# Other element orders for the feed-forward operands of a two-layer transformer kernel

## The chip, the cores and the metric

The kernel runs on one core of one Trainium2 chip. The metric is the device time of one execution in microseconds (us). Below, TensorE is the matrix engine (PE in the profile; PEld is its loading of weights, which overlaps its products), VectorE is DVE, ScalarE is ACT, GpSimd is POOL, and SyncE (SP) issues the transfers.

## The reference

Two layers over 512 tokens of width 1024. Layer 0 mixes tokens by attention over the best keys of an indexer, layer 1 by attention with compressed queries and keys. After each mixer comes the part that the change touches:

```python
def conv_ffn(h, w_up, conv_w, conv_b, w_down):      # h: 512 x 1024
    u = h @ w_up                                     # 512 x 5632
    u = conv_b + sum(conv_w[j] * up[:, j:j + S] for j in range(3))   # three taps along the tokens
    gate, val = jnp.split(u, 2, axis=-1)
    return (jax.nn.silu(gate) * val) @ w_down        # 2816 x 1024
```

All data are 32-bit floats.

## The kernel before

Activations lie with features on the 128 partitions and the 512 tokens along the free dimension. A product must keep more digits than the matrix engine's quick 32-bit form has, so each operand is split in two: an upper part (`w_hi`, `h_hi`, `a_hi`), which ScalarE makes by copying into that form, and a lower part (`w_lo`, `h_lo`, `a_lo`), which VectorE makes by subtracting the upper part from the original. `product3` (L1715 to L1717) then issues three matmuls for one tile, upper by upper, upper by lower and lower by upper, each with its own load of 128x128 weights and 512 moving columns.

Weights arrive in units in two slots of `raw` (SyncE's queue, L389). `hi(u)` (L571) on ScalarE waits for the transfer and for the slot's last use by TensorE, and copies `raw` to `w_hi`. `lo(u)` (L937) on VectorE follows it. TensorE waits for `w_lo_done`. SyncE's load of unit u into `raw` waits until `lo` of unit u - 2 is done.

The feed-forward part of layer `l` has two stretches:

- The up stretch, `feed_forward(l)`: 11 steps. A step takes two units of 2048 words a partition (8 blocks `k` of 256 columns, that is two tiles of 128 for each `k`), and makes four banks of `ps` (`channels`, q = 0 to 3) of 24 matmuls each. VectorE scales each bank (L1165), ScalarE and VectorE apply the taps (L786, L1172, L1177), ScalarE the silu (L807), and VectorE multiplies (L1198). In the middle steps, `hi` and `lo` of the next step's slot 0 stand behind the scaling of banks 0 and 1, those of slot 1 behind the rest of the step. The first step is written apart.
- The down stretch, `onto_residual(n, ...)` with n = 1 in layer 0 and n = 3 in layer 1: 22 units of 1024 words a partition, 8 tiles each; `tile_product` for tile `d` goes to bank `d`, so a unit has 24 matmuls. For each later unit ScalarE makes `w_hi` and `a_hi` (L733) as soon as unit u - 2 is used (`r_used`), VectorE `w_lo` and `a_lo` (L1106), and TensorE waits for both lower parts before the unit's first product.

Behind the last unit of the down stretch of layer 0, ScalarE waits for the transfer of the next stage's weights (`raw<-in_b_w_down`) and converts their second half (L761), VectorE subtracts it (L1135), and in program order behind that stand VectorE's additions of the eight banks to `xT` (L1139) and the next stage's features (`h_hi` L579, `h_lo` L943).

Of the kernel before, what the change touches and what calls it, by code (L numbers as in the profile page):

```python
# [21 lines left out]
F32 = mybir.dt.float32  # L22
F32R = mybir.dt.float32r
BF16 = mybir.dt.bfloat16
ALU = mybir.AluOpType
# [3 lines left out]
P = 128  # L29
# [86 lines left out]
def unit_words(u):  # L116

    if u < U_AOUT:
        return 4 * A_CHUNKS[(u - U_A) // 2][1]
    if u < U_UP[0]:  # L120
        return D
    if u < U_DOWN[0]:
        return SLOT
    if u < U_B:
        return D
    if u < U_BOUT:
        return (4 * B_DOWN, 4 * B_DOWN, QW, QW, D, D)[u - U_B]
    if u < U_UP[1]:
        return D
    return SLOT if u < U_DOWN[1] else D  # L130


def score_bank(u, e):
# [30 lines left out]
def hybrid_layers_kernel(nc, xt, vectors, t5_bias, a_in_wide, a_in_small, a_w_out, b_w_down, b_w_uq,  # L164
# [4 lines left out]
    with ExitStack() as ctx:  # L169
# [391 lines left out]
        def _(sc):  # L561
            chain = Chain(sc, act_seq)

            def hi(u, free=None, n=None, k=None):
# [187 lines left out]
            def onto_residual(n, u0, tiles, n_next, gain_at, nxt):  # L752

                with sc.Fori(0, tiles // 2 - 1) as i:
                    for b in range(2):
                        hi(u0 + 2 * i + b + 2, (r_used[n], 2 * i + b + 1), D, b)
                        act_hi(n, 2 * i + b + 2, b, False)
                if n_next < 4:
                    half = unit_words(nxt) // 2
                    sc.wait_ge(w_raw[0], 8 * nxt + 16)  # L760
                    sc.activation(w_hi[:, 0, D:D + half], raw[:, 0, D:D + half], ACT.Copy).then_inc(w_hi_upper, 1)  # L761
                    order = ORDER[n_next]
                    for j, k in enumerate(order):
                        features_hi(n_next, k, gain_at)
                        if j >= 2:
                            square_of(n_next, order[j - 2])
                        if j == KD - 2:
                            hi(nxt, (r_done[n], KD), half)
                    for k in order[-2:]:
                        square_of(n_next, k)  # L770
                    hi(nxt + 1, (r_done[n], KD))
                    if nxt == U_B:
                        table(ACT.Sqrt)
                        hi(U_B + 2, (pb_half, 1))
                    root_of_mean(n_next)

            def feed_forward(l):
                n = 2 * l + 1

                def tap2(i, q, first):  # L780

                    ch = l * CT + (q // 2) * FT + 2 * i + q % 2
                    sc.wait_ge(f_in[l], 4 * i + q + 1)
                    if not first:
                        sc.wait_ge(f_act[l], 2 * i)
                    sc.activation(cv[:, q, :], u_in[:, q, 2:2 + S], ACT.Identity,  # L786
                                  bias=conv[:, 3, bass.ds(ch, 1)], scale=conv[:, 2, bass.ds(ch, 1)])\
                        .then_inc(f_t2[l], 1)

                def step(i, first=False, last=False):  # L790
                    if first:
                        hi(U_UP[l] + 2, (f_done[l], 2))
                        sc.wait_ge(bc_ok, l + 1)
                        sc.activation(rbc[:], ps[:, 1, :], ACT.Copy).then_inc(rbc_ok, 1)
                    tap2(i, 0, first)
                    tap2(i, 1, first)
                    if first:
                        pass
                    elif last:
                        hi(U_DOWN[l], (f_done[l], 4 * i + 2))  # L800
                        act_hi(n, 0, 0, True)
                        act_hi(n, 1, 1, True)
                    else:
                        hi(U_UP[l] + 2 * i + 2, (f_done[l], 4 * i + 2), SLOT, 0)
                    for q in range(2):
                        sc.wait_ge(f_t0[l], 4 * i + q + 1)
                        sc.activation(cv[:, q, :], cv[:, q, :], ACT.Silu).then_inc(f_silu[l], 1)  # L807
                    tap2(i, 2, first)
                    tap2(i, 3, first)
                    if last:  # L810
                        hi(U_DOWN[l] + 1, (f_done[l], 4 * i + 4))
                    else:
                        hi(U_UP[l] + 2 * i + 3, (f_done[l], 4 * i + 4), SLOT, 1)
# [110 lines left out]
        def _(dve):  # L924
            chain = Chain(dve, dve_seq)

            def lo(u, n=None, k=None):
# [9 lines left out]
                dve.tensor_tensor(w_lo[:, s, 0:n], raw[:, s, 0:n], w_hi[:, s, 0:n].bitcast(F32), ALU.subtract)\  # L937
                    .then_inc(w_lo_done, 1)

            def prepare_lo(n, k, gain_at):  # L940

# [184 lines left out]
            def onto_residual(n, u0, tiles, n_next, gain_at, nxt):  # L1126
                with dve.Fori(0, tiles // 2 - 1) as i:
                    for b in range(2):
                        lo(u0 + 2 * i + b + 2, D, b)
# [21 lines left out]
            def feed_forward(l):  # L1151
                n = 2 * l + 1
                for t in range(T):
                    dve.tensor_scalar(diag[:, t, :], ident, rstd[:, t:t + 1], None, ALU.mult)\
                        .then_inc(diag_ok, 1)
                lo(U_UP[l] + 2)
                chain.then_wait(dve.memset(u_in[:, :, 0:2], 0.0))
                dve.wait_ge(rbc_ok, l + 1)

# [20 lines left out]
                def ffn_step(i, first=False, last=False):  # L1180
                    scaled(i, 0, first)
                    scaled(i, 1, first)
                    if first:
                        pass
                    elif last:
                        lo(U_DOWN[l])
                        act_lo(n, 0, 0)
                        act_lo(n, 1, 1)
                    else:
                        lo(U_UP[l] + 2 * i + 2, SLOT, 0)  # L1190
                    taps(i, (0, 1))
                    scaled(i, 2, first)
                    scaled(i, 3, first)
                    taps(i, (2, 3))
                    dve.wait_ge(f_t0[l], 4 * i + 4)
                    for q in range(2):
                        dve.wait_ge(f_silu[l], 2 * i + q + 1)
                        dve.tensor_tensor(act[:, 2 * i + q, :], cv[:, q, :], cv[:, 2 + q, :], ALU.mult)\  # L1198
                            .then_inc(f_act[l], 1)
                    if last:  # L1200
                        lo(U_DOWN[l] + 1)
                    else:
                        lo(U_UP[l] + 2 * i + 3, SLOT, 1)

                ffn_step(0, first=True)
                with dve.Fori(1, UP_STEPS - 1) as i:
# [114 lines left out]
        def _(pe):  # L1321
# [176 lines left out]
                if j == 2:  # L1498
                    ins.then_inc(o_ok[n], 1)

            def tile_product(d, b, start, stop):
# [26 lines left out]
            def onto_residual(n, u0, tiles):  # L1528

                def rows(i, first=False):  # L1530
                    for b in range(2):
                        pe.wait_ge(w_lo_done, u0 + 2 * i + b + 1)
                        pe.wait_ge(r_lo[n], 2 * i + b + 1)
                        for d in range(KD) if n % 2 or not first else (4, 5, 6, 7):
# [7 lines left out]
                            ins = tile_product(d, b, first and b == 0, False)  # L1542
                        ins.then_inc(r_used[n], 1)

                rows(0, first=True)
# [3 lines left out]
                pe.wait_ge(w_lo_done, u0 + tiles - 1)  # L1549
                pe.wait_ge(r_lo[n], tiles - 1)  # L1550
                for d in ORDER[n + 1][:AHEAD]:
                    tile_product(d, 0, False, False)
                pe.wait_ge(w_lo_done, u0 + tiles)
                pe.wait_ge(r_lo[n], tiles)
                for j, d in enumerate(ORDER[n + 1]):
                    if j >= AHEAD:
                        tile_product(d, 0, False, False)
                    tile_product(d, 1, False, True).then_inc(r_done[n], 1)

            def feed_forward(l):  # L1560
                n = 2 * l + 1

                def channels(i, q, first):
# [4 lines left out]
                        pe.wait_ge(f_in[l], 4 * i + q - 3)  # L1568
                    for k in range(KD):
                        cols = slice(k * 2 * P + part * P, k * 2 * P + (part + 1) * P)  # L1570
                        ins = product3(pe, ps[:, 4 + q, :], w_hi[:, s, cols], w_lo[:, s, cols], h_hi[:, k, :],
                                       h_lo[:, k, :], k == 0, k == KD - 1)
                    ins.then_inc(f_done[l], 1)


# [208 lines left out]
```

## Time and profile before

| | |
|---|---|
| time, median of 3 runs | 1264.58 us (1263.28 to 1265.5) |
| span of the profiled execution, first to last instruction | 1259.6 us |
| mean granted TensorE clock of it | 0.996 of full speed |
| busy: PE, PEld | 1220.7 us (97%), 980.3 us (78%) |
| busy: DVE, ACT, POOL | 767.4 us (61%), 547.5 us (43%), 212.6 us (17%) |
| up stretches, layer 0 and layer 1 | about 324 to 561 us, 899 to 1135 us of the span |
| down stretches, layer 0 and layer 1 | about 561 to 682 us, 1135 to 1256 us |

The page gives the profiled execution's span and no time of its own beside it. The span is 5.0 us under the median of the runs; that difference is what lies before the first and behind the last instruction, and is taken as fixed. A matmul's busy time in the profile includes the time that its results take to drain, so consecutive matmuls overlap, and the distance between their starts is the pace.

### The profile page before, as it was taken

The numbers are of one execution on the slowest core, as the hardware profiler recorded it, in microseconds if no ns is written. First come the engines' busy times: TensorE is split into PE (matmuls) and PEld (weight loads), VectorE is DVE, ScalarE is ACT, GpSimd is POOL, SyncE is SP. The second block draws the span as 40 slices with busy tenths as digits, with TensorE's granted clock in tenths as the row PEclk, the third lists the DMA queues.
The fourth block names the chain that finished last, engine by engine and source line by source line (L and its number), as shares of the span: only waits on it lengthen the run. The fifth ranks groups of instructions, "written<-read, shape, count | busy, mean of one in ns | idle before, by whom it ended". The sixth has DMA issues, their size and how long they took to land.

```text
span 1259.6 us, 17234 instructions
## 1 busy us (share of the span) xinstructions
PE 1220.7 (97%) x6072; PEld 980.3 (78%) x6080; DVE 767.4 (61%) x1337; ACT 547.5 (43%) x933; POOL 212.6 (17%) x262
## 2 busy tenths in 40 slices
PE   6999999999999999999999878999999999999998
PEld 4868886678788888888888766768788888887887
DVE  3577895754766666563337678762775666664334
ACT  5554435653633333332325676652543333343232
POOL 4314243430400000000003572430400000000000
PEclk9999999999999999999999999999999999999999
DMA  6432212204222232213332110012322222222323
GB/s 232 155 98 87 96 68 68 73 29 134 100 100 100 76 107 84 100 50 100 100 100 97 59 35 1 1 35 90 113 99 100 100 100 100 74 75 84 100 89 111
DMA packets 25120, 110.83 MB, mean 88 GB/s; under 512 B 2752, under 2 KB 3136, under 8 KB 17776
## 3 DMA queue, kind: packets, MB, share of 16 engines
q1 hardware_dynamic: 25072, 110.21, 25.8%
q8 instruction: 28, 0.46, 0.1%
q14 instruction: 20, 0.16, 0.0%
HBM read 108.06 MB, written 6.33 MB: 91 GB/s over the span
## 4 chain that ended last, share of the span: by engine, by line
PE 86%; DVE 6%; POOL 2%; ACT 2%; issue 2%; DMA 1%; SPq 0%; DVEq 0%; ACTq 0%; POOLq 0%
PE ps L1715 24%; PE ps L1717 24%; PE ps L1716 24%; PE ps L1476 3%; PE ps L1495 3%; PE ps L1376 2%; PE ps L1364 2%; DVE h_lo L943 1%; DVE xT L1139 1%; PE ps L1459 1%; DVE w_lo L937 1%; PE ps L1449 1%; PE ps L1359 1%; DMA xT<-in_xt 1%; POOL rope_tmp L479 1%
## 5 line engine op out<-in xcount | busy, mean ns | idle before, releaser
L937 DVE TENSOR_TENSOR w_lo<-raw,w_hi 128x1024 fp32r<-128x1024 f32 (+4 forms) x114 | 194.7, 1708 | 255.1 <-ACT w_hi L571 255.1
L1715 PE MATMUL ps<-h_hi,w_hi 128*128 128x512 f32 (+1 forms) x712 | 278.4, 391 | 2.4 <-DVE w_lo L937 2.4
L1716 PE MATMUL ps<-h_lo,w_hi 128*128 128x512 f32 (+1 forms) x712 | 277.7, 390 | 0.0
L571 ACT ACTIVATE w_hi<-raw 128x1024 fp32r<-128x1024 f32 (+4 forms) x124 | 177.7, 1433 | 229.8 <-PE ps L1717 229.5
L1717 PE MATMUL ps<-h_hi,w_lo 128*128 128x512 f32 (+1 forms) x712 | 277.5, 390 | 0.0
L1715 PE MATMUL ps<-a_hi,w_hi 128*128 128x512 f32 x480 | 188.0, 392 | 2.1 <-DVE w_lo L937 1.5
L1716 PE MATMUL ps<-a_lo,w_hi 128*128 128x512 f32 x480 | 186.8, 389 | 0.0
L1717 PE MATMUL ps<-a_hi,w_lo 128*128 128x512 f32 x480 | 186.8, 389 | 0.0
L1715 PEld LDWEIGHTS ps<-h_hi,w_hi 128*128 128x128 f32 (+1 forms) x712 | 133.5, 188 | 31.8 <-DVE w_lo L937 3.2
L1717 PEld LDWEIGHTS ps<-h_hi,w_lo 128*128 128x128 f32 (+1 forms) x712 | 133.6, 188 | 28.6 <-issue 0.6
L1716 PEld LDWEIGHTS ps<-h_lo,w_hi 128*128 128x128 f32 (+1 forms) x712 | 133.6, 188 | 28.1 <-issue 0.4
L786 ACT ACTIVATE cv<-u_in,vec 128x512 f32<-128x512 f32 x88 | 71.5, 816 | 187.4 <-DVE u_in L1165 185.4
L501 POOL TENSOR_TENSOR v<-v 128x512 f32<-128x512 f32 x28 | 50.7, 1810 | 462.5 <-ACT v L583 442.6
L1165 DVE TENSOR_TENSOR u_in<-ps,rbc 128x512 f32<-128x512 f32 x88 | 60.2, 688 | 94.3 <-PE ps L1717 91.5
L1715 PEld LDWEIGHTS ps<-a_hi,w_hi 128*128 128x128 f32 x480 | 90.1, 188 | 23.8 <-DVE w_lo L937 2.4
L1717 PEld LDWEIGHTS ps<-a_hi,w_lo 128*128 128x128 f32 x480 | 90.1, 188 | 18.8
L1716 PEld LDWEIGHTS ps<-a_lo,w_hi 128*128 128x128 f32 x480 | 90.1, 188 | 18.3
L1715 PE MATMUL ps<-w_hi,h_hi 128*128 128x512 f32 (+1 forms) x256 | 102.0, 398 | 2.4 <-DVE w_lo L937 1.9
L1717 PE MATMUL ps<-w_hi,h_lo 128*128 128x512 f32 (+1 forms) x256 | 99.5, 389 | 0.0
L1716 PE MATMUL ps<-w_lo,h_hi 128*128 128x512 f32 (+1 forms) x256 | 99.0, 387 | 0.0
L520 POOL TENSOR_SCALAR probs<-probs,inv_sum 128x256 f32<-128x256 f32 (+3 forms) x128 | 66.8, 538 | 106.7 <-DVE inv_sum L1024 106.5
L664 ACT ACTIVATE probs<-probs,neg_max 128x256 f32<-128x256 f32 (+3 forms) x128 | 70.5, 553 | 18.6 <-DVE neg_max L1014 18.4
(189 smaller groups left out, 1525.3 us busy)
## 6 DMA issues: line engine op xcount, KB each, us to landing
raw<-in_f_up SPq DMA_DIRECT2D x44, 1024.0 KB, 4.8
raw<-in_f_w_down SPq DMA_DIRECT2D x44, 512.0 KB, 3.4
raw<-in_a_in_wide SPq DMA_DIRECT2D x13, 1024.0 KB, 4.9
bias_tiles<-bias_rows SPq DMA_DIRECT2D x1, 4096.0 KB, 20.1
raw<-in_a_w_out SPq DMA_DIRECT2D x8, 512.0 KB, 3.4
raw<-in_b_w_out SPq DMA_DIRECT2D x8, 512.0 KB, 3.4
xT<-in_xt SPq DMA_DIRECT2D x4, 512.0 KB, 6.3
toep_b<-bias_tiles SPq DMA_DIRECT2D x8, 256.0 KB, 2.8
```

The costliest lines, as they stand in the source:

```text
L501: pool.tensor_tensor(total, total, sq[:, ORDER[n][k], :], ALU.add).then_inc(sq_sum, 1)
L520: ins = pool.tensor_scalar(x, x, inv_sum[:, slot, e, p:p + 1], 1.0, ALU.mult, ALU.mult)
L571: sc.activation(w_hi[:, s, 0:n], raw[:, s, 0:n], ACT.Copy).then_inc(w_hi_done, 1)
L664: ins = sc.activation(x, x, ACT.Exp, bias=neg_max[:, slot, e, p:p + 1], scale=-1.0, accum_out=sums[:, slot, e, p:p + 1])
L786: sc.activation(cv[:, q, :], u_in[:, q, 2:2 + S], ACT.Identity, bias=conv[:, 3, bass.ds(ch, 1)], scale=conv[:, 2, bass.ds(ch, 1)])\
L937: dve.tensor_tensor(w_lo[:, s, 0:n], raw[:, s, 0:n], w_hi[:, s, 0:n].bitcast(F32), ALU.subtract)\
L1165: dve.tensor_tensor(u_in[:, q, 2:2 + S], ps[:, 4 + q, :], rbc[:], ALU.mult).then_inc(f_in[l], 1)
L1476: ins = pe.transpose(ps[:, turn_bank(u, e), c * P:(c + 1) * P], probs[slot][:, e, c * P:(c + 1) * P], ident)
L1495: ins = pe.matmul(ps[e * DH:(e + 1) * DH, 7, b * P:(b + 1) * P], v[:, kb, h * DH:(h + 1) * DH], probsT[u % 2][:, e, c * P:(c + 1) * P], st ...
L1715: pe.matmul(dst, s_hi, m_hi, start=start, stop=False)
L1716: pe.matmul(dst, s_hi, m_lo, start=False, stop=False)
L1717: return pe.matmul(dst, s_lo, m_hi, start=False, stop=stop)
```

## The change

Three of the four feed-forward stretches read or write their operands in another order. The numbers computed are the same, and the instructions are as many as before.

- Up stretch of layer 0, from the second step: each matmul walks its 512 moving columns from the last to the first, and the bank of `ps` as well.
- Down stretch of layer 0: `hi` and `lo` write `w_hi` and `w_lo` so that column c of tile d stands at word 8c + d. Both read `raw` in order; VectorE reads `w_hi` and writes `w_lo` 8 words apart, ScalarE writes `w_hi` 8 words apart, and TensorE loads each tile's 128 columns 8 words apart.
- Up stretch of layer 1, from the second step: the two tiles of each block k are interleaved, so that column c of tile h stands at word 2c + h of the block. The same accesses are 2 words apart.
- Down stretch of layer 1, first steps of both up stretches, and all else: unchanged.

```diff
+def by_eights(x):
+    return x.rearrange("p (c d) -> p d c", d=KD)
+def by_pairs(x):
+    return x.rearrange("p (k c h) -> p k h c", h=2, c=P)
+def as_stored(x):
+    return x.rearrange("p (k h c) -> p k h c", h=2, c=P)
+def tiles_of(x):
+    return x.rearrange("p (a c) -> p a c", c=P)
+def down_view(n):
+    return (by_eights, tiles_of) if n == 1 else (None, None)
+def up_view(l):
+    return (by_pairs, as_stored) if l == 1 else (None, None)
...
             def hi(u, free=None, n=None, k=None, view=None, of=None):
...
-                sc.activation(w_hi[:, s, 0:n], raw[:, s, 0:n], ACT.Copy).then_inc(w_hi_done, 1)
+                to, source = w_hi[:, s, 0:n], raw[:, s, 0:n]
+                if view is not None:
+                    to, source = view(to), of(source)
+                sc.activation(to, source, ACT.Copy).then_inc(w_hi_done, 1)
...
             def lo(u, n=None, k=None, view=None, of=None):
...
+                to, source, less = w_lo[:, s, 0:n], raw[:, s, 0:n], w_hi[:, s, 0:n].bitcast(F32)
+                if view is not None:
+                    to, source, less = view(to), of(source), view(less)
+                dve.tensor_tensor(to, source, less, ALU.subtract).then_inc(w_lo_done, 1)
...
             def tile_product(d, b, start, stop, n=0):
                 cols = slice(d * P, (d + 1) * P)
+                if n == 1:
+                    cols = slice(d, D, KD)
...
                     for k in range(KD):
                         cols = slice(k * 2 * P + part * P, k * 2 * P + (part + 1) * P)
+                        if l == 1 and not first:
+                            cols = slice(k * 2 * P + part, (k + 1) * 2 * P, 2)
+                        bank, h_upper, h_lower = ps[:, 4 + q, :], h_hi[:, k, :], h_lo[:, k, :]
+                        if l == 0 and not first:
+                            bank, h_upper, h_lower = bank[:, ::-1], h_upper[:, ::-1], h_lower[:, ::-1]
```

The calls of `hi` and `lo` for the units of these stretches pass `*down_view(n)` or `*up_view(l)`.

## Rows read from the trace of the kernel before

**Rows 1.** The page: busy time by engine, and granted TensorE clock in 40 slices.

```profile
PE 1220.7 (97%) x6072; PEld 980.3 (78%) x6080; DVE 767.4 (61%) x1337; ACT 547.5 (43%) x933; POOL 212.6 (17%) x262
...
PEclk9999999999999999999999999999999999999999
```

**Rows 2.** The chain that ended last, shares of the span by engine.

```profile
PE 86%; DVE 6%; POOL 2%; ACT 2%; issue 2%; DMA 1%; SPq 0%; DVEq 0%; ACTq 0%; POOLq 0%
```

**Rows 3.** Windows within the three changed stretches: busy (count), clock, DMA, GB/s.

```profile
346.50:550.50 204.00, 204.00 (x902) 168.92 (x901) 129.12 (x151) 74.91 (x74) 0.00 (x0) 1.00 0.27 93
567.50:659.50 92.00, 92.00 (x406) 76.16 (x407) 31.06 (x34) 26.11 (x34) 0.00 (x0) 1.00 0.32 100
920.90:1124.90 204.00, 204.00 (x902) 168.92 (x901) 129.12 (x151) 74.90 (x74) 0.00 (x0) 1.00 0.26 93
```

**Rows 4.** Timeline, end of one down unit: start, duration, instruction.

```profile
605.48 0.39 PE L1717 MATMUL ps<-a_hi,w_lo 128*128 128x512 f32 x1
605.48 0.19 PEld L1715 LDWEIGHTS ps<-a_hi,w_hi 128*128 128x128 f32 x1
605.70 0.39 PE L1715 MATMUL ps<-a_hi,w_hi 128*128 128x512 f32 x1
```

**Rows 5.** Timeline, matmuls of 384 moving columns at full clock.

```profile
722.51 0.33 PE L1715 MATMUL ps<-w_hi,cq_hi 128*128 128x384 f32 x1
722.68 0.33 PE L1716 MATMUL ps<-w_lo,cq_hi 128*128 128x384 f32 x1
```

**Rows 6.** Timeline, eight weight loads whose matmuls have one column.

```profile
30.78 0.97 PEld L1329 LDWEIGHTS ps<-ones,v 128*128 128x128 f32 x8 [2.00 <-issue]
```

**Rows 7.** Timeline, matmuls of 416 columns while the granted clock was halved.

```profile
689.87 0.55 PE L1717 MATMUL ps<-w_hi,h_lo 128*128 128x416 f32 x1
690.22 0.55 PE L1715 MATMUL ps<-w_hi,h_hi 128*128 128x416 f32 x1
```

**Rows 8.** Groups by line and form: busy us, mean ns, idle before.

```profile
L937 DVE TENSOR_TENSOR w_lo<-raw,w_hi 128x2048 fp32r<-128x2048 f32 x45 | 105.4, 2342 | 58.0 <-ACT w_hi L571 58.0
L571 ACT ACTIVATE w_hi<-raw 128x2048 fp32r<-128x2048 f32 x55 | 104.7, 1904 | 23.3 <-PE ps L1717 23.0 <-DVE rstd L949 0.2
...
L937 DVE TENSOR_TENSOR w_lo<-raw,w_hi 128x1024 fp32r<-128x1024 f32 x63 | 79.8, 1267 | 193.6 <-ACT w_hi L571 193.6
...
L571 ACT ACTIVATE w_hi<-raw 128x1024 fp32r<-128x1024 f32 x63 | 66.7, 1059 | 202.4 <-PE ps L1717 202.4
...
L527 POOL TENSOR_TENSOR w_lo<-raw,w_hi 128x2048 fp32r<-128x2048 f32 x10 | 46.1, 4610 | 90.9 <-ACT w_hi L571 90.9
```

**Rows 9.** Timeline, conversion of one down unit of layer 0.

```profile
600.46 1.06 ACT L571 ACTIVATE w_hi<-raw 128x1024 fp32r<-128x1024 f32 x1 [3.80 <-PE ps L1717]
...
602.70 0.69 DVE L1106 TENSOR_TENSOR a_lo<-act,a_hi 128x512 fp32r<-128x512 f32 x1
```

**Rows 10.** Timeline, the second unit of the down stretch of layer 0.

```profile
566.20 1.22 DVE L937 TENSOR_TENSOR w_lo<-raw,w_hi 128x1024 fp32r<-128x1024 f32 x1
...
567.47 0.50 PE L1715 MATMUL ps<-a_hi,w_hi 128*128 128x512 f32 x1 [0.77 <-DVE w_lo L937]
```

**Rows 11.** The chain in order of time, end of the down stretch of layer 0.

```profile
665.74 1.07 ACT w_hi L571
...
666.84 1.24 DVE w_lo L937
...
668.09 5.22 DMA raw<-in_b_w_down
...
674.27 1.03 DVE w_lo L1135
```

**Rows 12.** Timeline, slot 1 in a middle step of an up stretch.

```profile
436.08 2.29 DVE L937 TENSOR_TENSOR w_lo<-raw,w_hi 128x2048 fp32r<-128x2048 f32 x1
...
441.19 0.19 PEld L1715 LDWEIGHTS ps<-h_hi,w_hi 128*128 128x128 f32 x1
```

More of the change, by code:

```diff
@@ L562, in _, with hi @@
             chain = Chain(sc, act_seq)
-            def hi(u, free=None, n=None, k=None):
+            def hi(u, free=None, n=None, k=None, view=None, of=None):
                 s = u % 2 if k is None else k
@@ L791, in step @@
                     if first:
-                        hi(U_UP[l] + 2, (f_done[l], 2))
+                        hi(U_UP[l] + 2, (f_done[l], 2), None, None, *up_view(l))
                         sc.wait_ge(bc_ok, l + 1)
@@ L810, in step @@
                     if last:
-                        hi(U_DOWN[l] + 1, (f_done[l], 4 * i + 4))
+                        hi(U_DOWN[l] + 1, (f_done[l], 4 * i + 4), None, None, *down_view(n))
                     else:
-                        hi(U_UP[l] + 2 * i + 3, (f_done[l], 4 * i + 4), SLOT, 1)
+                        hi(U_UP[l] + 2 * i + 3, (f_done[l], 4 * i + 4), SLOT, 1, *up_view(l))
                 step(0, first=True)
@@ L925, in _, with lo @@
             chain = Chain(dve, dve_seq)
-            def lo(u, n=None, k=None):
+            def lo(u, n=None, k=None, view=None, of=None):
                 if isinstance(u, int):
@@ L1155, in feed_forward @@
                         .then_inc(diag_ok, 1)
-                lo(U_UP[l] + 2)
+                lo(U_UP[l] + 2, None, None, *up_view(l))
                 chain.then_wait(dve.memset(u_in[:, :, 0:2], 0.0))
@@ L1185, in ffn_step @@
                     elif last:
-                        lo(U_DOWN[l])
+                        lo(U_DOWN[l], None, None, *down_view(n))
                         act_lo(n, 0, 0)
@@ L1189, in ffn_step @@
                     else:
-                        lo(U_UP[l] + 2 * i + 2, SLOT, 0)
+                        lo(U_UP[l] + 2 * i + 2, SLOT, 0, *up_view(l))
                     taps(i, (0, 1))
@@ L1200, in ffn_step @@
                     if last:
-                        lo(U_DOWN[l] + 1)
+                        lo(U_DOWN[l] + 1, None, None, *down_view(n))
                     else:
-                        lo(U_UP[l] + 2 * i + 3, SLOT, 1)
+                        lo(U_UP[l] + 2 * i + 3, SLOT, 1, *up_view(l))
                 ffn_step(0, first=True)
@@ L1541, in rows @@
                                 pe.wait_ge(f_in[n // 2], 2 * FT)
-                            ins = tile_product(d, b, first and b == 0, False)
+                            ins = tile_product(d, b, first and b == 0, False, n)
                         ins.then_inc(r_used[n], 1)
@@ L1551, in onto_residual @@
                 for d in ORDER[n + 1][:AHEAD]:
-                    tile_product(d, 0, False, False)
+                    tile_product(d, 0, False, False, n)
                 pe.wait_ge(w_lo_done, u0 + tiles)
@@ L1556, in onto_residual @@
                     if j >= AHEAD:
-                        tile_product(d, 0, False, False)
-                    tile_product(d, 1, False, True).then_inc(r_done[n], 1)
+                        tile_product(d, 0, False, False, n)
+                    tile_product(d, 1, False, True, n).then_inc(r_done[n], 1)
             def feed_forward(l):
@@ L1570, in channels @@
                         cols = slice(k * 2 * P + part * P, k * 2 * P + (part + 1) * P)
-                        ins = product3(pe, ps[:, 4 + q, :], w_hi[:, s, cols], w_lo[:, s, cols], h_hi[:, k, :],
-                                       h_lo[:, k, :], k == 0, k == KD - 1)
+                        if l == 1 and not first:
[3 more added lines that the diff above has]
+                            bank, h_upper, h_lower = bank[:, ::-1], h_upper[:, ::-1], h_lower[:, ::-1]
+                        ins = product3(pe, bank, w_hi[:, s, cols], w_lo[:, s, cols], h_upper, h_lower, k == 0,
+                                       k == KD - 1)
                     ins.then_inc(f_done[l], 1)
```

12 lines of the change are left out of this document (5 added, 7 removed).

## The prediction

> **What bounds the kernel now.** I first read the page's busy times and its clock row. TensorE is busy for 97% of the span at the upper level of its clock, 2.4 GHz [rows 1]. The chain that ended last says the same: 86% of it is TensorE [rows 2]. I then asked for windows inside the three changed stretches. TensorE is busy without a gap in each, VectorE 63% of the time in an up stretch and 34% in the down stretch, ScalarE less [rows 3]. So a layout can cost time in two ways only: it slows the matmuls or their loads, which all lie on the path, or it slows ScalarE's and VectorE's conversions so far that TensorE waits.
>
> The pace of TensorE is the distance between two starts: 605.70 - 605.48, read over a window as 92.0 us / 406 = 0.227 us [rows 3, 4]. With 384 columns it is about 0.173 us [rows 5], so a column costs (0.227 - 0.173) / 128 = 0.42 ns and 512 of them 0.216 us. About 0.01 us is left, which does not depend on the columns. The loads run beside this. Eight loads whose matmuls have a single column take 0.97 us, the last of them 0.19 us long: (0.97 - 0.19) / 7 = 0.111 us for a load of 128 columns when nothing else sets the pace [rows 6]. A load therefore has half of each 0.227 us to spare.
>
> **The change, part by part.** No instruction is added. No operand in this kernel's on-chip work is read or written backward or with single words apart, so the trace has no row for any of the three patterns, and each is bounded from rows.
>
> *Backward walk, layer 0 up.* Ten steps of 4 banks of 24 matmuls are 960. Lower bound: nothing, if the same words in the opposite order come at the same pace. Upper bound: one word where two came before. The nearest row is the stretch at half clock, where starts lie 0.35 us apart for 416 columns, 0.84 ns a column [rows 7]. That is twice 0.42 ns, so +0.216 us a matmul and 960 x 0.216 = +207 us. I take nothing: every word is still next to the one before it, and the row nearest in kind is the forward walk of the same words. No gain can come of it beyond the 0.01 us above.
>
> *Loads 8 words apart, layer 0 down.* 22 units of 24 are 528 loads. If the load takes as long as now, or even twice as long (0.223 us), it stays under 0.227 us and costs nothing [rows 4, 6]. Three times is 0.334 us, +0.107 us each, +57 us; four times 0.445 us, +115 us. I take at most twice, so 0, knowing that only 0.004 us is left over.
>
> The Trainium skill (Advanced Engine Details and Errata, section Memory Cachelines) says that on-chip memory is read in lines of 16 bytes, that at least two accesses must fall in one line to hide its latency, and that one line per access costs something; it gives no figure for it. No row here shows that. It is a warning about the 8-word pattern for all three engines and leaves out the 2-word one.
>
> *Conversions 8 words apart, layer 0 down.* ScalarE takes 1904 ns for 2048 words and 1059 ns for 1024, so 0.825 ns a word; VectorE 2342 and 1267 ns, so 1.05 ns [rows 8]. Lower bound: unchanged. For the upper side the only other price of this subtraction is GpSimd's, 4610 ns for 2048 words, twice VectorE's [rows 8]. I take twice a word's time on both: +0.84 us for `hi`, +1.07 us for `lo` (between unchanged and twice I choose twice, since each access leaves the words beside it unused; this is a choice, not a reading). In the steady units this is hidden, barely. Now `hi` starts at 600.46 and `a_lo` ends at 603.39 [rows 9]; the later times of the change are 603.39 + 0.84 + 1.07 = 605.30, and the first load of the unit stands at 605.48 [rows 4]. What remains is 0.2 us a unit. Two places have no such cover:
>
> - The second unit. TensorE already waits for its `w_lo`, 0.77 us, and `hi` was done long before [rows 10]. A longer `lo` goes straight on the path: +1.1 us.
> - The last-but-one unit. There the chain is `hi`, `lo`, then the transfer for the next stage into the slot just freed, then L761 and L1135, behind which VectorE's additions stand [rows 11]. `hi` and `lo` both count: +1.9 us. The additions and features after it run back to back on VectorE, so nothing gives it back.
>
> *Two words apart, layer 1 up.* Loads: even doubled they would hide as above. Conversions: unchanged at the lower bound. At the upper bound, doubled, `hi` of 2048 words takes 1.7 us more and `lo` 2.15 us more, twice a step. VectorE would be late by 3.8 us after slot 0, make up 1.7 us of it in its wait before the last bank, and end slot 1's `lo` at 438.4 + 2.1 + 2.1 = 442.6 where TensorE's load wants it at 441.19 [rows 12]: 1.4 us a step, +14 us over ten. I take nothing, as two words apart is nearer to the rows (one apart) than eight.
>
> *Sum.* 0 + 0 + 1.1 + 1.9 + 0 = +3.0 us on the profiled span of 1259.6 us, so 1262.6 us. The span stands 5.0 us under the median of the runs; 1264.6 + 3.0 = **1267.6 us**.
>
> **The rivals.**
>
> *No cost at all.* If ScalarE and VectorE do not notice the spacing either, the sum is 0: 1264.6 us. The rows speak neither for nor against it. It is also what comes of any edit that has no effect in the hardware.
>
> *A small miss.* Three mechanisms lie close. If the 0.01 us that is left over in the pace comes on top of a doubled load, the pace is 0.236 us and 528 x 0.009 = +5 us. If the conversions exceed double, the 0.2 us of cover in each of 20 units is used up, and each further 0.1 us costs 2 us. If 2-word writes are charged, up to +14 us. Together with the +3.0 this is 1269 to 1283 us.
>
> *Loads take over the down stretch.* Above 2.04 times their present 0.111 us they set the pace. With three to four times it is 1267.6 + 57 to 115 = 1325 to 1383 us. Against it: nothing in the rows. For it: the margin is 2%.
>
> *The backward walk halves the pace.* 1267.6 + 207 = 1475 us. This needs an engine that takes words in pairs only forward. The walk at 0.42 ns a word is twice as fast as any other engine's stream here (0.825 and 1.05 ns, and 0.84 ns for a load, rows 6 and 8), so it is where pairs would be needed. The Trainium skill (the same page and section) says of the matmul's results that every two in succession should be adjacent and that an order that is not contiguous slows matmuls significantly; by that the backward bank is at risk, if "contiguous" means ascending. No row here shows it.
>
> *Both, or something worse.* Over 1480 us.
>
> *Faster.* If part of the 0.01 us beside the columns came from loads and walk reaching for the same words' neighbourhood, another order could free it: up to 528 x 0.01 = 5 us. Nothing points to it.
>
> **How the numbers follow.** Forecast 0.27; no cost 0.16; small miss 0.16; loads 0.12; backward 0.20; both or worse 0.07; faster 0.02. The forecast is the likeliest single case, with a range of its own of 1265.5 to 1269.5 us. To hold 8 in 10 the range must reach the backward walk, since all cases below it hold only 0.71 to 0.73. So it is 1263.5 to 1477 us. The bound of 0.2% is 2.5 us. Slower by more: two thirds of the forecast's case (0.18), and all of the small miss, loads, backward and both (0.55), 0.73. Within: no cost and the rest of the forecast's, 0.25. Faster 0.02.
>
> **What would show each step.** The backward walk: the count of matmuls in a 204 us window of layer 0's up stretch, 902 now [rows 3], 460 if halved, with the granted clock still 1.00. The loads: the count in the down window, 406 now, and the duration of a load beside it, 0.19 us [rows 4]; with a doubled load about 0.3 us and the pace unchanged. The conversions: L571 of 1024 words at 1.9 us and L937 at 2.3 us in layer 0's down stretch, 1.06 and 1.23 us still in layer 1's. The two stalls: TensorE's wait of 0.77 us at the second unit grown to 1.8 us, and 1.9 us more between the last-but-one unit's use and the first `xT` addition. Two words apart: L571 and L937 of 2048 words in layer 1 as in layer 0. The prediction is wrong if TensorE's pace changes in any stretch, or if the steady units of the down stretch show a wait for `w_lo`.

## The result

The changed kernel takes 1285.78 us (median of four runs, 1283.84 to 1287.76) where the kernel before takes 1263.93 us (median of four, the three of the table above and one more). The ratio is 1.0175, 95% interval 1.0162 to 1.0189: slower by 1.6 to 1.9%. The profiled spans are 1282.1 and 1259.6 us, 22.5 us apart. In each run that has both on record the time is about 1.8 us above the span (1283.84 over 1282.1 here). The 5.0 us of the section on the time before set one execution's span beside the median of others; the differences used below do not depend on it.

The page of the changed kernel, busy times, chain and clock, answers to [rows 1, 2]:

```profile
PE 1243.5 (97%) x6080; PEld 1015.2 (79%) x6080; DVE 791.1 (62%) x1337; ACT 574.4 (45%) x933; POOL 212.6 (17%) x262
...
PEclk9999999999999999999999999999999999999999
...
PE 88%; DVE 6%; POOL 2%; issue 2%; ACT 1%; DMA 0%; SPq 0%; DVEq 0%; ACTq 0%; POOLq 0%
```

TensorE issues as many matmuls as before (the profile before lacks 8 of the 6080 records) and is busy 22.8 us longer (1243.5 - 1220.7), at the same clock. So most of the time is in its pace. Windows of the four stretches of the changed kernel (busy us and count by engine, granted clock, DMA share, GB/s), for layer 0 up, layer 0 down, layer 1 up, layer 1 down:

```profile
350.00:550.00 200.00, 200.00 (x859) 161.15 (x858) 122.00 (x144) 73.20 (x72) 0.00 (x0) 1.00 0.26 92
580.00:680.00 100.00, 100.00 (x410) 100.00 (x410) 48.53 (x34) 45.17 (x34) 0.00 (x0) 1.00 0.26 86
945.00:1145.00 200.00, 200.00 (x859) 165.44 (x858) 123.85 (x144) 76.38 (x72) 0.00 (x0) 1.00 0.25 89
1165.00:1265.00 100.00, 100.00 (x443) 82.79 (x442) 33.90 (x38) 28.60 (x37) 0.00 (x0) 1.00 0.30 100
```

The second number in each line is TensorE's: in none of these windows is it idle. The count tells the pace. The unchanged stretch makes 443 matmuls in 100 us, 0.227 us each, as [rows 3] have it. The backward stretch and the one with operands 2 words apart (the pairs) both make 859 in 200 us, 0.233 us; the one with operands 8 words apart (the eights) makes 410 in 100 us, 0.244 us. In the down stretch of layer 0 the loads (the third number) are busy for all of the window. From the starts of the matmuls one after the other the means are 226.67 ns in the unchanged stretch, 233.33 backward, 233.33 for the pairs and 244.67 for the eights.

The same stretches by line, changed kernel; first layer 0 down, then layer 1 up (count | busy us, mean ns | idle before), answering to [rows 8]:

```profile
L1759 PEld LDWEIGHTS ps<-a_hi,w_lo 128*128 128x128 f32 x150 | 49.7, 331 | 0.0
...
L973 DVE TENSOR_TENSOR w_lo<-raw,w_hi 128x1024 fp32r<-128x1024 f32 x19 | 43.1, 2268 | 59.1 <-ACT w_hi L604 59.1
L604 ACT ACTIVATE w_hi<-raw 128x1024 fp32r<-128x1024 f32 x19 | 42.3, 2229 | 62.9 <-PE ps L1759 62.9
...
L1757 PEld LDWEIGHTS ps<-h_hi,w_hi 128*128 128x128 f32 x279 | 53.8, 193 | 11.3
...
L973 DVE TENSOR_TENSOR w_lo<-raw,w_hi 128x2048 fp32r<-128x2048 f32 x17 | 38.9, 2290 | 26.7 <-ACT w_hi L604 26.7
L604 ACT ACTIVATE w_hi<-raw 128x2048 fp32r<-128x2048 f32 x18 | 37.3, 2072 | 0.0
```

A load 8 words apart is recorded at 331 ns against 188, one 2 words apart at 193. The conversions 8 words apart have about doubled. Those 2 words apart cost ScalarE 9% and VectorE nothing. Timeline of the changed kernel at the two ends of the down stretch of layer 0 (in brackets the idle time before and what ended it), answering to [rows 10, 11]:

```profile
574.47 0.64 PE L1757 MATMUL ps<-a_hi,w_hi 128*128 128x512 f32 x1 [1.21 <-DVE w_lo L973]
...
690.84 0.68 DVE L1141 TENSOR_TENSOR a_lo<-act,a_hi 128x512 fp32r<-128x512 f32 x1
...
691.67 0.60 PE L1757 MATMUL ps<-a_hi,w_hi 128*128 128x512 f32 x1 [1.56 <-DVE a_lo L1141]
...
692.80 1.42 DVE L1174 TENSOR_TENSOR xT<-xT,ps 128x512 f32<-128x512 f32 x2 [0.34 <-PE ps L1759]
```

The first wait was 0.77 us and is 1.21. The second is new: the last unit's `a_lo` is late, and TensorE, which by then has only five tiles of the unit before (15 matmuls) to work on, waits 1.56 us for it. VectorE's additions to `xT` (last line) then wait 0.34 us for TensorE, not the other way round.

**Where the 22.5 us are.** Up stretch of layer 0: 960 x 6.67 ns = 6.4 us. Down stretch of layer 0: it runs from its first to its last matmul in 120.6 us before and 132.5 us after, +11.9; 528 x 18.0 ns = 9.5 us of that is pace, the rest the two waits. The stage behind it is 2.0 us shorter (162.96 us before, 161.00 after, from last to first matmul of the stretches beside it), all of it within its first 14 us. TensorE's wait there is shorter, and behind it the granted clock was at its lower level, 1.2 GHz, for 3.4 us before [rows 7] and not after. The lines are that wait before, then in the changed kernel:

```profile
688.48 0.45 PE L1715 MATMUL ps<-w_hi,h_hi 128*128 128x416 f32 x1 [1.93 <-DVE w_lo L937]
...
706.02 0.46 PE L1757 MATMUL ps<-w_hi,h_hi 128*128 128x416 f32 x1 [1.40 <-DVE w_lo L973]
```

This gain of 2.0 us goes with the late conversions. Of the kernels of the next section the eights alone gain 2.0 us at this place and the conversions alone 1.5 us, both without the drop of the clock; the backward walk alone, the pairs alone and the loads alone have the drop and gain nothing. Why the drop stays away is open. Up stretch of layer 1: 6.4 us. The sum, 6.4 + 11.9 - 2.0 + 6.4 = 22.7 us, agrees with 22.5.

### The profile page after: what moved, and what is told of

The parts are those of the page before. It is cut to its first block, busy times and chain, and to the rows that moved or that the text cites. A ratio compares the mean times of both kernels' runs of the same rounds, so it can differ in the third digit from the quotient of the medians.

```text
span 1282.1 us, 17242 instructions
## 1 busy us (share of the span) xinstructions
PE 1243.5 (97%) x6080; PEld 1015.2 (79%) x6080; DVE 791.1 (62%) x1337; ACT 574.4 (45%) x933; POOL 212.6 (17%) x262
## 4 chain that ended last, share of the span: by engine, by line
PE 88%; DVE 6%; POOL 2%; issue 2%; ACT 1%; DMA 0%; SPq 0%; DVEq 0%; ACTq 0%; POOLq 0%
PE ps L1757 25%; PE ps L1759 24%; PE ps L1758 24%; PE ps L1511 3%; PE ps L1530 3%; PE ps L1411 2%; PE ps L1399 2%; DVE h_lo L978 1%; DVE xT L1174 1%; PE ps L1494 1%; DVE w_lo L973 1%; PE ps L1394 1%; PE ps L1484 1%; POOL rope_tmp L509 1%; PE ps L1729 1%
## 5 line engine op out<-in xcount | busy, mean ns | idle before, releaser
L973 DVE TENSOR_TENSOR w_lo<-raw,w_hi 128x1024 fp32r<-128x1024 f32 (+4 forms) x114 | 218.2, 1914 | 245.3 <-ACT w_hi L604 245.2
L604 ACT ACTIVATE w_hi<-raw 128x1024 fp32r<-128x1024 f32 (+4 forms) x124 | 206.6, 1666 | 215.9 <-PE ps L1759 215.7
L1757 PE MATMUL ps<-h_hi,w_hi 128*128 128x512 f32 (+1 forms) x712 | 283.1, 398 | 2.4 <-DVE w_lo L973 2.4
L1758 PE MATMUL ps<-h_lo,w_hi 128*128 128x512 f32 (+1 forms) x712 | 282.4, 397 | 0.0
L1759 PE MATMUL ps<-h_hi,w_lo 128*128 128x512 f32 (+1 forms) x712 | 282.3, 396 | 0.0
L1757 PE MATMUL ps<-a_hi,w_hi 128*128 128x512 f32 x480 | 191.4, 399 | 4.1 <-DVE a_lo L1141 2.2
L1758 PE MATMUL ps<-a_lo,w_hi 128*128 128x512 f32 x480 | 190.3, 396 | 0.0
L1757 PEld LDWEIGHTS ps<-a_hi,w_hi 128*128 128x128 f32 x480 | 114.9, 239 | 18.9 <-DVE w_lo L973 4.6
L1759 PEld LDWEIGHTS ps<-a_hi,w_lo 128*128 128x128 f32 x480 | 115.3, 240 | 12.1
L1758 PEld LDWEIGHTS ps<-a_lo,w_hi 128*128 128x128 f32 x480 | 115.2, 240 | 11.5
```

Source lines behind the costliest of these rows:

```text
L604: sc.activation(to, source, ACT.Copy).then_inc(w_hi_done, 1)
L973: dve.tensor_tensor(to, source, less, ALU.subtract).then_inc(w_lo_done, 1)
L1757: pe.matmul(dst, s_hi, m_hi, start=start, stop=False)
L1758: pe.matmul(dst, s_hi, m_lo, start=False, stop=False)
L1759: return pe.matmul(dst, s_lo, m_hi, start=False, stop=stop)
```

## The experiments

**One pattern at a time.** The first three kernels keep one pattern each and set the others back, as this for the first:

```diff
-    return (by_eights, tiles_of) if n == 1 else (None, None)
+    return (None, None)
-    return (by_pairs, as_stored) if l == 1 else (None, None)
+    return (None, None)
-                if n == 1:
-                    cols = slice(d, D, KD)
-                        if l == 1 and not first:
-                            cols = slice(k * 2 * P + part, (k + 1) * 2 * P, 2)
```

> Theory A (each pattern costs TensorE a small amount per matmul, and the amounts add): the pace in the middle steps of layer 0's up stretch is 233.3 ns against 226.7, all other stretches are at 226.7; 960 x 6.67 ns = +6.4 us, so 1270 us. Rival B (the pace rises through something the three edits share, such as the longer program or more crowded memory): with two of three edits gone the backward stretch loses some or all of its 6.67 ns, and the time is 1264 to 1268 us.

Measured: 1.0048 of the kernel before (1.0032 to 1.0063), 1269.23 us. The pace is 233.33 ns in the backward stretch and 226.67 elsewhere. Windows of layer 0's up and down stretches:

```profile
350.00:550.00 200.00, 200.00 (x859) 161.15 (x858) 122.03 (x144) 73.23 (x72) 0.00 (x0) 1.00 0.26 92
580.00:680.00 100.00, 100.00 (x443) 82.79 (x442) 34.50 (x38) 29.39 (x38) 0.00 (x0) 1.00 0.30 98
```

> Theory A: the pace of layer 0's down stretch is 244.7 ns, elsewhere 226.7; 528 x 18.0 ns = +9.5 us, and two stalls of 0.4 us at the second unit and about 1.7 us at the last, less up to 2 us that the next stage may give back: 1273 to 1276 us. Rival B: the pace is nearer to 226.7 ns with the other edits gone.

Measured: 1.0069 (1.0052 to 1.0086), 1272.16 us, 0.8 us under the expected range. The pace is 244.2 ns in layer 0's down stretch, 226.67 elsewhere. Window of layer 0's down stretch:

```profile
580.00:680.00 100.00, 100.00 (x411) 100.00 (x411) 48.62 (x35) 45.52 (x34) 0.00 (x0) 1.00 0.28 89
```

> Theory A: the pace in the middle steps of layer 1's up stretch is 233.3 ns, elsewhere 226.7; +6.4 us, 1270 us, no new stalls. Rival B: 1264 to 1267 us.

Measured: 1.0056 (1.0039 to 1.0073), 1269.76 us. The pace is 233.3 ns in layer 1's up stretch, 226.67 elsewhere. Window of layer 1's up stretch:

```profile
945.00:1145.00 200.00, 200.00 (x859) 165.43 (x858) 122.65 (x145) 74.80 (x75) 0.00 (x0) 1.00 0.25 87
```

The three add up, 0.48 + 0.69 + 0.56 = 1.73% against 1.75%, each known to 0.15 to 0.17%. Theory A stands, rival B falls: each pattern pays in its own stretch, whatever the others do.

**Loads or conversions.** This kernel spaces only TensorE's loads. It and the six kernels after it compute something else than the reference (other columns or tokens, or a part of them) and ran once each, so they are read for paces and durations within their profiles more than for their times.

```diff
+                        if l == 0 and not first:
+                            at = 4 * P * (k // 2) + 2 * (k % 2) + part
+                            cols = slice(at, 4 * P * (k // 2 + 1), 4)
                         if l == 1 and not first:
+                            cols = slice(2 * k + part, SLOT, 16)
...
+                if n == 3:
+                    cols = slice(2 * P * (d // 2) + d % 2, 2 * P * (d // 2 + 1), 2)
```

> The conversions write in order and the walks are forward; only the loads are spaced: 4 words in layer 0's up stretch, 8 in its down stretch, 16 in layer 1's up stretch, 2 in its down stretch. The products then take other weight columns than the reference. Theory C (the loads alone make the pace): 244.7 ns at 8 words and 233.3 at 2, with loads of 331 and 193 ns. If what counts is that each word is alone in a line of 16 bytes, 4, 8 and 16 words give one and the same pace, 244.7 ns; if the cost grows with the distance, 4 words lie between 233.3 and 244.7 and 16 above. Rival D (the spaced writes of ScalarE and VectorE crowd the memory that TensorE reads): all four stretches stay at 226.7 ns.

Measured: 1291.0 us. Windows of this kernel for 4, 8, 16 and 2 words:

```profile
350.00:550.00 200.00, 200.00 (x852) 200.00 (x852) 120.81 (x142) 73.32 (x72) 0.00 (x0) 1.00 0.26 92
580.00:680.00 100.00, 100.00 (x411) 100.00 (x410) 31.06 (x34) 26.86 (x34) 0.00 (x0) 1.00 0.27 89
945.00:1145.00 200.00, 200.00 (x847) 200.00 (x846) 121.36 (x143) 72.54 (x71) 0.00 (x0) 1.00 0.25 90
1165.00:1265.00 100.00, 99.39 (x426) 81.91 (x426) 34.31 (x39) 28.18 (x36) 0.00 (x0) 1.00 0.28 95
```

The mean distances are 235.0, 244.7, 236.5 and 233.3 ns, the last outside a wait in its window. So the loads alone make the pace, and rival D falls. Neither form of theory C holds as written. From 2 to 4 words the recorded load jumps from 193 to 310 ns; it is 331 ns at 8 and 300 ns at 16. That step fits a load that is long once each word is alone in 16 bytes, but 8 words is worse than 4 and 16. Why 8 is worst stays open. The Trainium skill (Advanced Engine Details and Errata, section Memory Cachelines) says that on-chip memory has lines of 16 bytes and that at least two accesses must fall in one line to hide its latency; the step of the recorded load between 2 and 4 words is where it puts it, and the further difference between 4, 8 and 16 is not in it. For moving columns it does not hold: two of them 2 words apart share a line, and they already double a matmul, as measured below.

This kernel also prices the waits: its down stretch of layer 0 takes 129.7 us against the changed kernel's 132.5, so the late conversions there cost 2.8 us.

**Is the load itself the bound?** Two kernels narrow the matmuls, leaving out the other columns of each bank.

```diff
+                        if not first:
+                            bank, h_upper, h_lower = bank[:, 0:256], h_upper[:, 0:256], h_lower[:, 0:256]
...
+                some = slice(0, 256 if n % 2 else S)
```

> The changed matmuls have 256 moving columns instead of 512 (half of each bank is left out). Layer 0 up: backward; layer 0 down: loads 8 words apart; layer 1 up: loads 2 words apart; layer 1 down: in order. In order the pace is 106.7 + 13.3 = 120 ns. If the cost of the backward walk is fixed per matmul, layer 0 up is at 126.7 ns; if it is by the column, 123.3. The same two numbers for loads 2 words apart. Loads 8 words apart: if a load takes 0.218 us by itself, that is now the pace, or a little more; if the cost was a fixed 18 ns, 138 ns.

Measured: 1133.19 us. The windows of layer 0 down (8 words) and layer 1 down (in order, with some waits of TensorE in it):

```profile
540.00:620.00 80.00, 80.00 (x334) 80.00 (x333) 25.57 (x28) 22.10 (x28) 0.00 (x0) 1.00 0.26 89
1080.00:1100.00 20.00, 19.41 (x157) 18.80 (x157) 12.14 (x14) 10.16 (x14) 0.00 (x0) 1.00 0.51 179
```

In order the distance between starts is 120 ns outside the waits, as expected. With loads 8 words apart it is 241 ns, though the matmul is half as wide. The load is the bound. It takes 241 ns by itself, not the 0.218 or 0.223 us of a plain doubling. Backward, 256 columns have a mean of 118.5 ns, and with loads 2 words apart 120.1 (both where TensorE neither waits nor is at the lower clock, which it is for short pieces of these two stretches): at this width neither costs anything.

The same with 64 columns and loads 4, 3, 16 and 1 words apart:

> The changed matmuls have 64 moving columns instead of 512 (the rest of each bank is left out), so that the loads set the pace, and the loads are 4 words apart in layer 0's up stretch, 3 words in its down stretch, 16 in layer 1's up stretch and in order in its down stretch; conversions are in order. In order: 0.111 us a load, as for one column. If a spaced load reads its 128 columns at half the pace, 4 and 16 words give 0.218 us, and the 235 to 245 ns of the full stretches are the load plus something of 17 to 27 ns. If 4 and 16 words give less than 0.15 us, the load is not the bound and the added 8 to 18 ns come from a clash with the moving columns. 3 words (two words in one line of four, then one) should lie between, near 0.165 us.

Measured: 1245.46 us. It does not settle what a load costs by itself at full clock, as its windows for 4, 3, 16 and 1 words show:

```profile
400.00:500.00 100.00, 100.00 (x430) 100.00 (x430) 60.68 (x71) 37.19 (x37) 0.00 (x0) 0.50 0.26 94
580.00:640.00 60.00, 60.00 (x283) 60.00 (x282) 21.91 (x24) 17.84 (x23) 0.00 (x0) 0.50 0.30 104
950.00:1050.00 100.00, 100.00 (x460) 100.00 (x459) 67.36 (x78) 38.85 (x38) 0.00 (x0) 0.50 0.26 94
1140.00:1200.00 60.00, 60.00 (x283) 60.00 (x282) 21.07 (x24) 17.83 (x23) 0.00 (x0) 0.50 0.31 105
```

The granted clock (third number from the end) is 0.50: TensorE fell to 1.2 GHz and stayed there for 327 and 314 us, while it issued loads and 64-column matmuls without a gap. So these paces aren't comparable with the others. Within the kernel they are: at half clock a load in order takes 213 ns, 3 words apart the same, 4 words 233 and 16 words 218.6. At full clock and 512 columns the paces at 4 and 16 words were 235.0 and 236.5 ns, so these loads take no longer at half the clock. That suggests that something other than TensorE's clock bounds them. It is not shown: what a load 4 or 16 words apart takes by itself at full clock was not measured, and loads 8 words apart were not run at half clock.

**Which walk costs.** One walk is changed in each stretch, all else in order:

```diff
                         if l == 0 and not first:
+                            h_upper, h_lower = h_upper[:, ::-1], h_lower[:, ::-1]
+                        if l == 1 and not first:
+                            bank, h_upper, h_lower = in_runs(bank, 2), apart(h_upper, 2), apart(h_lower, 2)
...
                 if n == 1:
+                    bank = bank[:, ::-1]
+                if n == 3:
+                    bank, a_upper, a_lower = in_runs(bank, 4), apart(a_upper, 4), apart(a_lower, 4)
```

> Everything is stored and loaded in order; one walk is changed in each stretch, so the outputs are those of tokens in another order. Layer 0 up: the moving columns backward, the bank forward. Layer 0 down: the bank backward, the moving columns forward. Layer 1 up: moving columns 2 words apart (even ones, then odd ones). Layer 1 down: moving columns 4 words apart. If the read of the moving columns costs the 6.67 ns of the backward stretch, layer 0 up is at 233.3 ns and layer 0 down at 226.7; if the write of the bank costs it, the other way round; if each costs half, 230 in both. If the moving read suffers from spacing as the loads do, 2 words cost little and 4 words (one word of each 16 bytes) up to double the pace, 440 ns; if it only suffers a fixed amount, both are at 233.3.

Measured: 1608.06 us. Windows in the order of the stretches:

```profile
350.00:550.00 200.00, 200.00 (x859) 161.12 (x858) 122.01 (x144) 73.24 (x72) 0.00 (x0) 1.00 0.26 92
580.00:680.00 100.00, 100.00 (x443) 82.84 (x442) 34.40 (x38) 30.12 (x39) 0.00 (x0) 1.00 0.29 98
950.00:1350.00 400.00, 400.00 (x884) 183.18 (x883) 131.00 (x152) 75.25 (x77) 0.00 (x0) 1.00 0.13 46
1400.00:1600.00 200.00, 200.00 (x435) 90.40 (x434) 35.18 (x40) 26.82 (x34) 0.00 (x0) 1.00 0.14 47
```

The read of the moving columns backward carries the whole 6.67 ns (859 in 200 us); a bank written backward is free (443 in 100 us). Moving columns 2 words apart double the pace exactly, 453.3 ns, and 4 words apart add little to that, 461.3 ns. That is a price for moving columns that the loads don't have: loads 2 words apart cost 6.67 ns. The four numbers fit a moving walk that takes two adjacent words at a time, in either direction. That reading was not tested further, for instance with pairs of words that lie apart.

**Two at once, and other widths.**

```diff
+                        if l == 0 and not first:
+                            cols = slice(k * 2 * P + part, (k + 1) * 2 * P, 2)
...
                         if l == 0 and not first:
+                            h_upper, h_lower = h_upper[:, ::-1], h_lower[:, ::-1]
+                        if l == 1 and not first:
+                            bank, h_upper, h_lower = bank[:, 0:384], h_upper[:, 0:384], h_lower[:, 0:384]
...
+                if n == 3:
+                    cols = slice(d, D, 8)
...
+                if n == 3:
+                    a_upper, a_lower = a_upper[:, ::-1], a_lower[:, ::-1]
```

> Conversions are in order, the products take other columns than the reference. Layer 0 up: moving columns backward and loads 2 words apart. If the two 6.67 ns are separate costs of one matmul the pace is 240.0 ns; if they are one cost that any order other than the plain one brings, 233.3. Layer 0 down: loads 3 words apart, forward. Layer 1 up: loads 8 words apart with 384 moving columns instead of 512. If the load is itself the bound, the pace stays at 241 to 245 ns although the matmul alone would need 173.3; if the 18 ns are an addition to the matmul, it is 191. Layer 1 down: loads 8 words apart and moving columns backward. If the load is the bound, 244.7 ns as without the backward walk; if costs add, 251.3.

Measured: 1298.44 us. Windows in the order of the stretches (the last has a wait in it):

```profile
360.00:560.00 200.00, 200.00 (x859) 169.01 (x858) 123.84 (x144) 72.04 (x72) 0.00 (x0) 1.00 0.25 89
580.00:680.00 100.00, 100.00 (x426) 100.00 (x425) 32.50 (x36) 28.44 (x36) 0.00 (x0) 1.00 0.27 92
945.00:1145.00 200.00, 200.00 (x825) 200.00 (x825) 120.48 (x142) 69.80 (x69) 0.00 (x0) 1.00 0.24 87
1165.00:1265.00 100.00, 99.80 (x402) 99.49 (x401) 32.30 (x37) 26.57 (x34) 0.00 (x0) 1.00 0.27 89
```

Backward and 2 words apart together are at 233.33 ns, not 240: not two costs. Loads 3 words apart are at 235.6 ns. Loads 8 words apart with 384 columns stay at 242.8 ns, where the matmul alone needs 173.3 [rows 5]: the load is the bound once more. With the moving columns backward beside it the 244.7 become 248.3 ns outside the wait, between the two expectations.

The last of the narrow kernels changes the widths in the same way (shown in part; its loads 2 words apart are made as above):

```diff
+                some = slice(0, {1: 384, 3: 448}.get(n, S))
...
+                            w = 384 if l == 0 else 448
+                            bank, h_upper, h_lower = bank[:, 0:w], h_upper[:, 0:w], h_lower[:, 0:w]
+                            h_upper, h_lower = h_upper[:, ::-1], h_lower[:, ::-1]
```

> Narrower matmuls, conversions in order. Layer 0 up: backward with 384 columns; layer 0 down: loads 2 words apart with 384 columns; layer 1 up: backward with 448 columns; layer 1 down: in order with 448 columns. In order, 448 columns should be at 186.7 + 13.3 = 200.0 ns and 384 at 173.3. If backward costs a fixed 6.67 ns, it is at 180.0 with 384 and 206.7 with 448; if it costs by the column, 178.3 and 205.8; with 256 columns it had vanished, so 173.3 and 200.0 would say that it belongs to 512 columns only. The same for loads 2 words apart: 180.0 or 173.3.

Measured: 1169.13 us. Windows in the order of the stretches:

```profile
360.00:510.00 150.00, 149.52 (x832) 147.04 (x831) 119.05 (x142) 67.96 (x69) 0.00 (x0) 1.00 0.32 115
545.00:605.00 60.00, 60.00 (x348) 60.00 (x347) 27.05 (x30) 22.25 (x29) 0.00 (x0) 1.00 0.36 122
880.00:1030.00 150.00, 150.00 (x727) 136.34 (x726) 102.65 (x119) 60.53 (x60) 0.00 (x0) 1.00 0.29 105
1090.00:1150.00 60.00, 60.00 (x298) 55.62 (x297) 21.92 (x24) 19.73 (x25) 0.00 (x0) 1.00 0.34 112
```

In order, 448 columns are at 202.6 ns (expected 200.0). Backward, 384 columns are at 177.8 (outside the waits) and 448 at 206.7: +4.5 and +4.1 ns. Loads 2 words apart with 384 columns are at 173.3: no cost. So the small cost is neither fixed nor by the column. Over the widths 256, 384, 448 and 512 backward costs -1.5, +4.5, +4.1 and +6.7 ns, pairs 0, 0, not run, and +6.7. The distances of single matmuls alternate between 176 and 182 ns in the backward stretch of 384 columns, between 202 and 211 in that of 448, and among 199, 202 and 207 in order with 448; backward with 512 they are all 233.3. That looks like a handover between load and matmul that happens only at certain instants, so that a small delay is rounded up at one width and lost at another. This is argued, not shown; what the small delay is stays open.

**The conversions alone.** Loads and walks in order, ScalarE and VectorE 4, 8, 16 and 2 words apart:

```diff
-    return (by_eights, tiles_of) if n == 1 else (None, None)
+    return (by_eights, tiles_of) if n == 1 else (two_apart, two_runs)
-    return (by_pairs, as_stored) if l == 1 else (None, None)
+    return (four_apart, four_runs) if l == 0 else (sixteen_apart, sixteen_runs)
```

> Only ScalarE's and VectorE's conversions are spaced (the products then take columns of several tiles): 4 words in layer 0's up stretch, 8 in its down stretch, 16 in layer 1's up stretch, 2 in its down stretch. TensorE loads in order, so its pace is 226.7 ns everywhere. If a spaced access costs double once each word is alone in its 16 bytes, hi of 2048 words takes about 3.6 us and lo about 4.4 us at 4 and at 16 words, hi of 1024 words 2.2 us and lo 2.3 us at 8, and at 2 words 1.15 and 1.23 us. Doubled conversions of 2048 words make TensorE wait at slot 1 of each middle step, by 1.4 us as worked out in the prediction, 14 us in each up stretch; with the 2 us at the ends of layer 0's down stretch the time is 1280 to 1295 us. If the price is lower at 4 than at 16 words, layer 0's up stretch shows shorter waits than layer 1's.

Measured: 1281.31 us. By line in the middle of layer 0's up stretch, 4 words apart, then TensorE's waits over the whole span (us in total, times, longest):

```profile
L634 ACT ACTIVATE w_hi<-raw 128x2048 fp32r<-128x2048 f32 x19 | 73.5, 3866 | 0.0
L1003 DVE TENSOR_TENSOR w_lo<-raw,w_hi 128x2048 fp32r<-128x2048 f32 x19 | 73.0, 3844 | 45.7 <-ACT w_hi L634 44.7
```

```profile
PE ps L1781 <- DVE w_lo L1003: 19.1, 26, 1.9
```

The time is 18.1 us above the 1263.2 us that the kernel before took beside it, in the expected range at its lower end. Each up stretch took 8.7 us longer than before, not 14, and layer 0's down stretch 3.1 us (123.7 against 120.6).

Both take about 3.85 us for 2048 words where 1.90 and 2.29 us stood [rows 8], at 4 and at 16 words alike; 1024 words 8 apart take 2.19 and 2.20 us; 2 words apart cost 6% on ScalarE, nothing on VectorE. So 2048 spaced words take about 1.9 ns each on both engines, the fixed part of an instruction included, against 0.93 and 1.12 ns in order. That is double for ScalarE and 1.7 times for VectorE. The pace of TensorE stays within 1 ns of 226.7 in the steady units of layer 0's down stretch, so spaced writes beside it do not slow the matmuls; conversions slow it only by being late. There they are not late:

```profile
580.00:680.00 100.00, 100.00 (x442) 82.12 (x441) 49.73 (x36) 47.23 (x36) 0.00 (x0) 1.00 0.28 95
```

## Why the prediction was right or wrong

The time lies in the range and slower was forecast, but the point, 1267.6 us, is 18 us short of 1285.8: +3.0 us was forecast and +21.9 measured. The range held it by its width alone, drawn for a halved pace that did not come. By the sign that the prediction itself gave for being wrong, a changed pace in any stretch, it was wrong in three stretches. The reading of what bounds the kernel held: all of the cost lies in TensorE's pace and in waits at the two ends of one stretch.

- **Backward walk.** Wrong in size. "I take nothing" measured +6.4 us. The rival of a halved pace, +207 us, did not come. The kernel that changes one walk in each stretch puts the whole cost on the read of the moving columns. The bank, at risk by the sentence of the Trainium skill (Advanced Engine Details and Errata, section Memory Cachelines) if an order that is not contiguous includes a backward one, costs nothing backward: 443 matmuls in 100 us, as in order.
- **Loads 8 words apart.** This is the step that failed most, +9.5 us for 0. The mechanism was the one named, a load that becomes the bound; the mis-sized term is the load. "At most twice", 0.223 us, measured 0.241 us by itself, and 0.244 with 512 columns beside it. The 0.004 us that was left over did not cover this. The rival had the threshold right and the size far too high, since I priced only whole multiples.
- **Loads 2 words apart.** Taken as nothing since a load has half of each matmul to spare. It measured +6.4 us though the recorded load grew only from 188 to 193 ns. The step that failed is the assumption that a load and a matmul beside it are independent until one is longer than the other.
- **Conversions 8 words apart.** Right in kind, by a choice and not a reading: 2.23 and 2.27 us against the 1.90 and 2.30 worked out, so ScalarE's term was 0.33 us too small. The steady units hid them, at the old pace too (442 matmuls in 100 us with the conversions alone).
- **Conversions 2 words apart.** Right, nothing on the path, though ScalarE's took 9% longer. The upper bound, 1.4 us a step for conversions that double, was too high: with words 4 and 16 apart it was about 0.9 us (8.7 us over ten steps), with VectorE's subtraction 1.6 us longer where 2.15 was assumed.
- **The stalls.** The second unit waits 0.4 us more, not 1.1: its `lo` took 2.08 us, and TensorE arrived 0.43 us later. At the end the path was another than forecast. The named chain, over the next stage's transfer to VectorE's additions, did not set the time: the additions waited 0.34 us for TensorE. What TensorE waited for, 1.56 us, was the last unit's own `a_lo`, late behind longer `hi` and `lo`. Nor does the step "nothing gives it back" hold: the next stage gave 2.0 us back. Together they cost 2.4 us (11.9 less 9.5) to 2.8 us (against the kernel with spaced loads alone), where 3.0 were forecast; with the conversions alone, at the old pace, they cost 3.1 us. So the size was near, for the end of the stretch by luck.
- **The rivals as cases.** The outcome lies in none: it is above the small miss (1269 to 1283 us) and below the loads' case (1325). Three patterns gave three small costs at once, and I had let each rival run by itself. The cost of a load, given as 0.84 ns a word, is 0.87 by [rows 6]; nothing rests on it.

## What to carry to other kernels

When TensorE is busy without a gap, count its matmuls in equal windows before and after: a change of 3% in the pace shows no wait anywhere. Keep the moving columns adjacent, since single words 2 apart already double a matmul; weight columns may lie apart at 3 to 8% with 512 moving columns, and a load 8 words apart needs 241 ns, so narrower matmuls wait for it. ScalarE and VectorE take about 1.9 ns for each word 4 or more apart (2048 words), which is free only while their work is not the last to arrive.

## What the runs showed of the hardware

- Moving columns: backward +6.67 ns for 512 columns, 2 words apart 453.3 ns, 4 words apart 461.3 ns, against 226.67 in order. A bank of results written backward: no cost.
- Loads of 128 columns by spacing of 1, 2, 3, 4, 8 and 16 words are recorded at 188, 193, 252, 310, 331 and 300 ns, and the pace with 512 columns is 226.7, 233.3, 235.6, 235.0, 244.7 and 236.5 ns.
- With 64-column matmuls and no gap on TensorE the granted clock was 0.50 in the windows of all four stretches, with loads in order too; with 256 columns and loads 8 words apart, also without a gap (80 of 80 us), it was 1.00.
